# mLSTM in a one-core encoder layer: keys and values fetched as 32x32 squares and turned on VectorE

## What is computed

```python
xn = rmsnorm(x, p['norm_mix_pre'])
proj = xn @ p['w_in']
q, k, v, o, ig, fg, u, gates = jnp.split(proj, SPLITS, axis=-1)
...
w = jnp.exp(logd - m_tok[..., None])
inter = jnp.exp(g - m_tok)
s = jnp.einsum('bjhd,bshd->bhjs', q, k) * w
num = jnp.einsum('bhjs,bshe->bjhe', s, v) + inter_blh[..., None] * jnp.einsum('bjhd,bhde->bjhe', q, C)
den = jnp.sum(s, axis=-1).transpose(0, 2, 1) + inter_blh * jnp.einsum('bjhd,bhd->bjh', q, n)
h = num / jnp.maximum(jnp.abs(den), floor)[..., None]
w_last = w[:, :, -1, :]
C_new = decay[..., None, None] * C + jnp.einsum('bhs,bshd,bshe->bhde', w_last, k, v)
n_new = decay[..., None] * n + jnp.einsum('bhs,bshd->bhd', w_last, k)
```

## Time and profile before

| | us |
|---|---|
| three executions, median | 1893.55 |
| lowest and highest | 1891.72 and 1895.24 |
| the profiled execution, its own time | 1891.67 |
| its span in the profile | 1889.9 |
| stage of the steps, start to end | about 572 to 845 |
| PE busy over the span | 1871.4 (99%) |
| granted TensorE clock, mean | 0.999 |

### The profile page before, as it was taken

The page is one execution under the profiler, slowest core; times in us unless marked ns, Lnnn a source line. Parts: engine busy times, 40 slices in busy tenths (PEclk is TensorE's granted clock), DMA queues, the critical chain, the costliest instruction groups (busy, mean ns, idle before and its releaser), DMA issues.

```text
span 1889.9 us, 33104 instructions
## 1 busy us (share of the span) xinstructions
PE 1871.4 (99%) x13219; PEld 1847.9 (98%) x13219; DVE 1331.9 (70%) x1975; ACT 873.5 (46%) x1601; POOL 110.5 (6%) x165
## 2 busy tenths in 40 slices
PE   9999999999999999999999999999999999999997
PEld 8999999999999999999999999999999999999997
DVE  7788999999997654783455479877776776636363
ACT  5554434544554456661222455644544454535342
POOL 0011111111111111110000000000000000000000
PEclk9999999999999999999999999999999999999999
DMA  4556676667656655559431341222121213556654
GB/s 136 160 141 150 161 190 167 158 176 184 191 165 203 203 156 159 156 167 242 123 140 45 120 138 67 81 70 91 69 81 69 92 69 128 177 204 203 213 171 158
DMA packets 155864, 272.86 MB, mean 144 GB/s; under 512 B 55997, under 2 KB 91837, under 8 KB 155713
## 3 DMA queue, kind: packets, MB, share of 16 engines
q1 hardware_dynamic: 140592, 235.16, 37.1%
q0 software_dynamic: 15120, 35.59, 10.6%
HBM read 206.97 MB, written 63.74 MB: 143 GB/s over the span
## 4 chain that ended last, share of the span: by engine, by line
PE 89%; DVE 5%; DMA 3%; issue 1%; ACT 1%; SPq 0%; POOL 0%; DVEq 0%; ACTq 0%; POOLq 0%
PE ps L1198 9%; PE ps L1200 9%; PE ps L1199 9%; PE ps L1352 7%; PE ps L1353 7%; PE ps L1354 7%; PE ps L1549 7%; PE ps L1547 7%; PE ps L1548 7%; PE ps L1569 4%; PE ps L1571 4%; PE ps L1570 4%; PE ps L1289 1%; PE ps L1286 1%; DMA araw<-wts 1%
## 5 line engine op out<-in xcount | busy, mean ns | idle before, releaser
L1198 PE MATMUL ps<-rx,fhi 128*128 128x368 f32 (+2 forms) x736 | 248.2, 337 | 0.8 <-ACT spl L1722 0.6
L1200 PE MATMUL ps<-rx,flo 128*128 128x368 f32 (+2 forms) x736 | 237.5, 323 | 0.0
L1199 PE MATMUL ps<-rx,fhi 128*128 128x368 f32 (+2 forms) x736 | 237.3, 322 | 0.0
L1352 PE MATMUL ps<-rx,ahi 128*128 128x304 f32 (+1 forms) x672 | 194.3, 289 | 0.4 <-DVE v L2570 0.3
L1353 PE MATMUL ps<-rx,ahi 128*128 128x304 f32 (+1 forms) x672 | 193.7, 288 | 0.0
L1354 PE MATMUL ps<-rx,alo 128*128 128x304 f32 (+1 forms) x672 | 193.6, 288 | 0.0
L1569 PE MATMUL ps<-ghi,dhi 128*128 128x384 f32 (+1 forms) x528 | 173.2, 328 | 2.7 <-DVE glo L2934 1.9
L1570 PE MATMUL ps<-glo,dhi 128*128 128x384 f32 (+1 forms) x528 | 172.3, 326 | 0.0
L1571 PE MATMUL ps<-ghi,dlo 128*128 128x384 f32 (+1 forms) x528 | 172.2, 326 | 0.0
L2927 DVE TENSOR_TENSOR dlo<-draw,dhi 128x1408 fp32r<-128x1408 f32 x48 | 77.8, 1624 | 118.3 <-ACT dhi L2136 118.3
L1198 PEld LDWEIGHTS ps<-rx,fhi 128*128 128x128 f32 x736 | 138.4, 188 | 2.8 <-ACT spl L1722 0.9
(11 more groups left out here) (364 smaller groups left out, 5701.8 us busy)
## 6 DMA issues: line engine op xcount, KB each, us to landing
draw<-wdn SPq DMA_DIRECT2D x48, 704.0 KB, 4.2
araw<-wts SPq DMA_DIRECT2D x105, 256.0 KB, 4.4
uraw<-wts SPq DMA_DIRECT2D x44, 512.0 KB, 4.3
fraw<-wts SPq DMA_DIRECT2D x27, 512.0 KB, 3.8
qkv<-scr_qkv SPq DMA_DIRECT2D x22, 544.0 KB, 8.9
scr_g<-cva SPq DMA_DIRECT2D x22, 512.0 KB, 2.6
alo<-wts POOLq DMA_DIRECT2D x42, 256.0 KB, 5.6
graw<-scr_g SPq DMA_DIRECT2D x43, 192.0 KB, 4.1
```

The costliest lines, as they stand in the source:

```text
L1198: pe.matmul(b, hi[:, w], src[:, his[k], cols], start=(k == 0), stop=False)
L1199: pe.matmul(b, hi[:, w], src[:, los[k], cols], start=False, stop=False)
L1200: mm = pe.matmul(b, lo[:, w], src[:, his[k], cols], start=False, stop=(k == KB - 1))
L1352: pe.matmul(b, ahi[s][:, c], bhi[:, k, :], start=(fresh and k == 0), stop=False, skip_group_check=True)
```

## The change

Keys and values no longer pass through TensorE. For each step SP loads k and v of its 128 tokens as 32x32 squares into a small buffer `kvq` (four DMAs of 32 partitions x 16 runs of 32 floats), one piece ahead of the step. DVE transposes all squares at once (`turn`, one STREAM_TRANSPOSE of 512 columns) into `kvt`, which holds k and v side by side; ACT multiplies the k half in place (`weighted_keys`), one piece later. The head's whole blocks 2 and 3 (v) are no longer loaded; `kvq` lies in their place in `qkv[0]`, and the order `C_HI` is altered to fit. The scores' matmuls move from the middle of a piece to the end of the piece before, behind the values. ACT's squares go to bank 2 instead of `zt`. The core of the diff:

```diff
-C_HI = (12, 14, 0, 2, 4, 6, 8, 10)
+C_HI = (12, 14, 0, 8, 4, 6, 2, 10)
...
+    kvq = [room(f"kvq{s}", [P, 16, 32]) for s in range(2)]
...
-    vt = [room(f"vt{s}", [P, VW]) for s in range(2)]
-    kw = [room(f"kw{s}", [P, DH]) for s in range(2)]
+    kvt = [room(f"kvt{s}", [P, DH + VW]) for s in range(2)]
...
-                for b in range(6):
+                for b in (0, 1, 4, 5):
                     sp.dma_start(qkv[h % 2][:, b, :], scr_qkv[h, b]).then_inc(qk_in, 16)
+
+            def load_squares(i):
+                h, j = STEPS[i]
+                at = step_cols(j).start
+                if i >= 2:
+                    sp.wait_ge(turned_set, i - 1)
+                for b in range(4):
+                    sp.dma_start(kvq[i % 2][32 * b:32 * b + 32, :, :],
+                                 scr_qkv[h, 0:4, :, at + 32 * b:at + 32 * b + 32].rearrange("k (a q) n -> q (k a) n", q=32))\
+                        .then_inc(kvq_in[i % 2], 16)
...
             for s, ((kind, k), c) in enumerate(SLOTS):
+                i = step_at(s, -1)
+                if i is not None:
+                    load_squares(i)
                 i = step_at(s, 1)
...
         def _(pe):
...
-                if i == 0:
-                    pe.wait_ge(gt_set, 5)
...
                 if i:
-                    pe.wait_ge(kv_copied, 2 * i)
                     pe.wait_ge(a_set, i)
-                for b in range(4):
-                    mm = pe.transpose(bank(2, b * P, P), q[:, b, cols], ident[:, :])
-                mm.then_inc(kv_full, 1)
                 for b in range(2):
                     mm = pe.matmul(bank(3, 0, L), q[:, b, cols], q[:, 4 + b, cols], start=(b == 0), stop=(b == 1))
...
                 i = step_at(s, 1)
                 if i is not None:
                     values(i)
+                i = step_at(s, -1)
+                if i is not None:
+                    scores(i)
...
         def _(act):
...
-                act.activation(vt[p][:, 0:DH], bank(2, DH, DH), ACT.Copy).then_inc(kv_copied, 1)
-                act.activation(kw[p][:, :], bank(2, 0, DH), ACT.Copy, scale=gt[:, 16 * j + 12 + h:16 * j + 13 + h])\
-                    .then_inc(kv_copied, 1)
...
+            def weighted_keys(i):
...
+                act.wait_ge(turned_set, i + 1)
+                act.activation(kvt[p][:, 0:DH], kvt[p][:, 0:DH], ACT.Copy, scale=gt[:, 16 * j + 12 + h:16 * j + 13 + h])\
+                    .then_inc(kw_set, 1)
...
+            def turn(i):
+                p = i % 2
+                if i >= 2:
+                    dve.wait_ge(n_full, i - 1)
+                dve.wait_ge(kvq_in[p], 32 + 64 * (i // 2 + 1))
+                dve.transpose(kvt[p][:, 0:2 * DH], kvq[p][:, :, :].rearrange("p a n -> p (a n)")).then_inc(turned_set, 1)
...
                     exponents(i)
                     scores(i)
+                    turn(i)
```

More of the change, by code:

```diff
@@ L786, in load_first_head @@
                 sp.wait_ge(grp_done, b_at(NB - 1, 3, 1))
-                for b in range(4):
+                for b in range(2):
                     sp.dma_start(qkv[0][:, b, :], scr_qkv[0, b]).then_inc(qk_in, 16)
@@ L794, in load_head, with store_head @@
                 else:
-                    sp.wait_ge(qk_in, 64 + 96 * (h - 1))
+                    sp.wait_ge(qk_in, 32 + 64 * (h - 1))
                     sp.wait_ge(nq_full, NSTEP * (h - 1))
-                for b in range(6):
+                for b in (0, 1, 4, 5):
                     sp.dma_start(qkv[h % 2][:, b, :], scr_qkv[h, b]).then_inc(qk_in, 16)
+            def load_squares(i):
[7 more added lines that the diff above has]
+                        .then_inc(kvq_in[i % 2], 16)
+            def store_head(i):
+                h, j = STEPS[i]
+                first = 0 if j < NCHUNK else L - DEC
+                sp.wait_ge(zs_set, i + 1)
+                sp.dma_start(scr_z[h, step_cols(j)][first:L], zs[i % 2][first:L, :]).then_inc(z_out[i % 2], 16)
             def pairs():
@@ L842, in pairs @@
                 weights(N_A + 2)
-            def store_head(i):
-                h, j = STEPS[i]
-                first = 0 if j < NCHUNK else L - DEC
-                sp.wait_ge(zs_set, i + 1)
-                sp.dma_start(scr_z[h, step_cols(j)][first:L], zs[i % 2][first:L, :]).then_inc(z_out[i % 2], 16)
             def load_nb(i):
@@ L948, in _ @@
                             sp.wait_ge(csq_set, KB + 2)
+                        elif C_HI[j] == 8:
+                            sp.wait_ge(gate_act, 6)
+                            sp.wait_ge(gate_dve, 16)
+                        elif C_HI[j] == 2:
+                            sp.wait_ge(turned_set, len(STEPS))
                         else:
@@ L1191, in _, with product @@
         def _(pe):
-            def product(b, hi, lo, rows, src, cols, at=0, halfway=None, his=range(KB), los=range(KB, 2 * KB)):
+            def product(b, hi, lo, rows, src, cols, his=range(KB), los=range(KB, 2 * KB)):
                 for k in range(KB):
@@ L1200, in product @@
                     mm = pe.matmul(b, lo[:, w], src[:, his[k], cols], start=False, stop=(k == KB - 1))
-                    if halfway is not None and k == at:
-                        halfway()
                 mm.then_inc(grp_done, 1)
@@ L1254, in scores @@
                 cols = step_cols(j)
[L1255 to L1256 removed]
                 if j == 0 and h == 0:
                     pe.wait_ge(t_free, EVAC_AT[last_slot("q", 2 * h + 1)])
[L1259 removed]
+                    pe.wait_ge(qk_in, 32)
                 elif j == 0:
[L1261 removed]
+                    pe.wait_ge(qk_in, 32 + 64 * h)
                 if i:
[L1263 removed]
                     pe.wait_ge(a_set, i)
[L1265 to L1267 removed]
                 for b in range(2):
@@ L1286, in values @@
                         pe.matmul(bank(5, 0, VW), qkv[h % 2][:, 4 + b, cols], c[:, b, :], start=(b == 0), stop=(b == 1))
-                pe.matmul(bank(4, 0, VW), wt[p][:, :], vt[p][:, :], start=True, stop=True).then_inc(nq_full, 1)
+                pe.matmul(bank(4, 0, VW), wt[p][:, :], vt, start=True, stop=True).then_inc(nq_full, 1)
                 for b in range(2):
-                    mm = pe.matmul(bank(6 + b, 0, VW), kw[p][:, b * P:(b + 1) * P], vt[p][:, :], start=True, stop=True)
+                    mm = pe.matmul(bank(6 + b, 0, VW), kvt[p][:, b * P:(b + 1) * P], vt, start=True, stop=True)
                 mm.then_inc(n_full, 1)
@@ L1388, in _ @@
                             pe.wait_ge(w_acc[n % 2], 16 * NB + ACC_IN[n])
-                    i = step_at(s, 0)
-                    rows, halfway = None, (lambda: scores(i)) if i is not None else None
+                    rows = None
                     if (kind, k) == START[0]:
@@ L1401, in _ @@
                     else:
-                        product(b, fhi[wslot(n)], flo[wslot(n)], rows, rx, cols_of(s), 3, halfway)
+                        product(b, fhi[wslot(n)], flo[wslot(n)], rows, rx, cols_of(s))
                     if s == 3:
@@ L1669, in values @@
                 act.wait_ge(hn_set, i + 1)
-                if i >= 2:
-                    act.wait_ge(zs_set, i - 1)
-                act.activation(zt[p][:, :], hn[p][:, 0:DH], ACT.Square, accum_out=sm[p][:, 3:4]).then_inc(ssq, 1)
+                if i:
+                    act.wait_ge(ssq, i)
+                act.activation(bank(2, 0, DH), hn[p][:, 0:DH], ACT.Square, accum_out=sm[p][:, 3:4]).then_inc(ssq, 1)
             def normed(i):
```

32 lines of the change are left out of this document (20 added, 12 removed).

## The result

| | before | after |
|---|---|---|
| median, us | 1892.63 (4 runs) | 1906.28 (4 runs) |
| lowest and highest | 1889.69 to 1895.24 | 1902.34 to 1908.35 |
| the profiled execution | 1891.67 | 1906.06 |
| its span | 1889.9 | 1904.3 |
| granted TensorE clock, mean | 0.999 | 0.995 |

The ratio is 1.0070, with a 95% interval of 1.0048 to 1.0093: 0.7% slower, 13.7 us. The forecast was 1884.5, faster, with a range of 1877 to 1899. Both its sign and its range missed.

A forecast was written before the change was run, and what follows sets the result against it. PE, busy 99% of the span, was taken as the bound: -17.5 us on PE, +4 for DVE in the last ten pieces and +4.5 for waits on loads gave -9, so 1884.5 us, range 1877 to 1899.

The forecast's parts named there:

- -15.8 for the transposes: On PE, four transposes fewer in each of 36 steps, at 0.44 us for four: -15.8 us.
- -0.7 for the scores' place: On PE, scores moved from mid-piece to behind the values save 0.02 us in each of 36 steps: -0.7 us.
- Costs nothing: At a piece's end, the moved scores' new wait for DVE's L2371 has over 3 us to spare: zero.
- The -1.0 of PE's first wait: At step 0, PE's wait for the gate columns passes to ACT, a piece later: -1.0 us.
- +4 for the last ten pieces: In the last ten pieces, DVE's lateness and waits around the store of `zs` stall PE: +4 us (0 to 8).
- 17 ns a packet: On the DMA engines, each 128-byte packet costs 17 ns, so a step's squares take 2.2 us of all engines.
- Share 0.82: In the stage with the steps, the DMA engines' busy share rises from 0.59 to about 0.82, which still fits.
- Squares land in 5 to 8 us: The squares' loads land in 5 to 8 us, within 10.8 us available, so most turns wait for nothing.
- Rival C: Squares land too late for the two-piece ring of turn, free, load, turn, making it slower: 1905 us; chance 0.17.
- Start, +1.5: At the start, DVE waits while both buffers fill with `scr_c`, `decs` and weights in flight: +1.5 us.
- Four issues at 0.43: On SP's queue, a step's four square loads issue at 0.43 us each; stores of `zs` go out 1.7 us later.
- Rival B: DVE's added work and its loads take the whole gain back, time within 3.8 us of before: 1892 us; chance 0.15.

The follow-up runs named there:

- the order mended: The change, with step 1's squares ahead of `decs` and the store of `zs` and `nb` ahead of the squares on SP's queue: 1883.57 us.
- long runs: The change, with each step's four loads bringing the same bytes in 512-byte runs instead of 128-byte squares: 1894.09 us.
- the start's edit: The change, with step 1's squares loaded ahead of the four `decs` broadcasts: 1900.68 us; store and `nb` ahead but without it: 1894.29 us.

## Why the prediction was wrong

- **-15.8 for the transposes: right.** 144 records fewer, undisturbed pieces at 6.60 to 6.63. So, as far as one profile can tell, was -0.7 for the scores' place by itself (0.6 in the intervals of the kernel before). The figure of about 275 ns that the prediction took from the Trainium skill (TensorE: Matmul & The Clock Gate, Part 4) stands there beside a figure for bf16; the fp32 transposes here last 272 ns in the median.
- **"Costs nothing", the new wait of the scores for L2371: wrong at the start.** It was worked out from a piece of the last ten (and took the start of L2371, 812.08, for its end, 0.3 later, which changes nothing). At step 0 and 1 DVE has the gate columns and four taps ahead: 2.9 us in the change, 2.3 where only the scores moved. The change's four other waits of this kind, 4.5 us, are gone with the order mended, so they belong to the late transfers. The -1.0 of PE's first wait came with it, so the two are +1.9 and not -1.0. In the end they mattered less, since the start is set by a landing.
- **DVE's 0.70 for `turn`: right** (701 ns). **+4 for the last ten pieces: right in size**, 5.5 in the change, 3.1 where the order is mended, and 3.1 there without squares' loads.
- **17 ns a packet: near** (13 to 15). **Share 0.82: near (0.78), but in part by luck.** The sum takes back 21 us for 16 blocks that are no longer loaded. The stage loads 12 whole blocks instead of 18, so it is 6 blocks and 8 us, and the sum should have given 0.87; the packets' lower price made up for it. **Squares land in 5 to 8 us: wrong to the good**, 3.1 in the median. DVE waited for them once. Rival C, whose time of 1905 came out, fell as a mechanism: the ring of turn, load, turn never ran dry after the start.
- **Start, +1.5: mis-sized.** It measured 10.0 in the first three intervals; with the order mended elsewhere, 9.2 without the start's edit and 0.2 with it. I listed `decs` and the weights as neighbours of the squares but did not look at how they stood on SP's queue, nor add that PE returns at half clock.
- **"Four issues at 0.43" (1.7 us), and "the stores of `zs` go out 1.7 us later", hidden in the light pieces: the step that failed.** A fixed price was put on an issue. The four took 1.9 to 9.1 us, the issue behind them as much as 4.3, and the store stood behind both and behind the wait for `turn`: 7.9 us behind its rows in the median instead of 0.95, so 7 us later and not 1.7. Even with long runs, whose four issues take 2.2 us, it was 3.8 us later: the wait for `turn`, which stands ahead of the four, has no term in the sum. That is the 12.9 us of the middle, of which 2.3 are left with the mended order, and part of the last ten. Nothing was priced for `nb`, which was the next to show.
- **Rival B** named the store's waits of 5.9 us, which are what grew (to 18.4), but gave them no price. With the order mended the time is 1883.6, near the forecast of 1884.5, but not term by term: the losses over the shrunken intervals are 5.7 us where the sum had 8.5, and up to some 2.5 us of the gain is the store's new place, which the sum didn't have.
- **The range** reached 1899, though the prediction's last line draws the line at 1889.8; the time lies beyond both.
- The prediction followed each added DMA to its landing, and not to what stands behind it on the queue.

What stays open: why the issue of one DMA takes several us. The rows show it where many short packets have been issued and not yet moved, and not with 512-byte runs. A high share isn't needed: `scr_ga`'s issue of 7.17 us begins at 577.47, where the share is under 0.1. That the queue is out of room is my reading, not shown. Open too is what makes the start's transfers land at 588 to 590 in every order; that it is POOL's burst was not tried.

## What to carry to other kernels

A queue that issues in program order is an engine like the others: for every DMA added, list what stands behind it and when that is due, and put the urgent small transfers (a store that frees a buffer, a row that an engine waits for) ahead of the bulk that has a piece to spare. When a wait is mended, look at once for the next in the same queue: three edits gave 9 us in two steps and 14 in the third. And price the first step apart from the steady state; that is where all the setting-up transfers are.

## What the runs showed of the hardware

- One DMA's issue on SP took up to 7.2 us (`scr_ga`) and 7.4 (a square's) when thousands of 128-byte packets were issued and not yet landed; in the kernel before `scr_ga` took at most 0.43 and a store of `zs` 0.44 in the median.
- A packet of 128 bytes costs an engine 13 to 15 ns, one of 512 bytes about 28: a quarter of the length at about half the price.
- Four broadcasts of 8 KB to 128 partitions kept the DMA share at 0.05 to 0.06, one engine of sixteen, for some 3 us, and the 64-KB loads issued behind them on the same queue landed some 12 us after their issue.
- Behind a gap of 7.6 us, PE's granted clock was 0.50 from 592 to 596 and 0.75 in the next 4 us, so the gap costs about 2 us beyond its own length (half of the 1.94 us busy in the one, a quarter of the 4 in the other). Behind a gap of 1.7 us at 654 the clock stayed at 1.00; behind one of 2.0 at 689 it was 0.77 and 0.80 for 4 us each, so the length of the gap alone doesn't tell. Nor does it in one place of two versions: behind the gap of 2.9 us at 576 the clock was 1.00 for the next 4 us in the change and 0.62 in the version with all three edits.
- One STREAM_TRANSPOSE of 512 columns takes 701 ns where 256 take 438.
